# A triangular inverse in 32x32 array tiles, with part of a convolution moved to ScalarE and GpSimd

## The reference

```python
m = jnp.where(strict, jnp.einsum('bhncd,bhnsd->bhncs', k_beta, k) * decay, 0.0)
rhs = jnp.concatenate([v_beta, k_beta * jnp.exp(g)[..., None]], axis=-1)
sol = lax.linalg.triangular_solve(m + jnp.eye(C, dtype=jnp.float32), rhs, left_side=True, lower=True,
                                  unit_diagonal=True)
u = sol[..., :Dv]
w = sol[..., Dv:]
```

```python
y = val * jax.nn.sigmoid(gate)
y = causal_depthwise_conv(y, dw) + dw_bias.astype(y.dtype)
mu = jnp.mean(y32, axis=-1, keepdims=True)
var = jnp.mean(jnp.square(y32 - mu), axis=-1, keepdims=True)
```

## Time and profile before

| | |
|---|---|
| median of 3 runs | 2652.47 us (2650.78 to 2653.61) |
| the profiled execution | 2650.35 us, its span 2648.6 us |
| TensorE matmuls | 2560.8 us busy, 97% of the span |
| TensorE weight loads | 2027.1 us, 77% |
| VectorE | 1530.4 us, 58% |
| ScalarE | 1089.3 us, 41% |
| GpSimd | 114.6 us, 4% |
| granted TensorE clock, mean | 0.987 |

### The profile page before, as it was taken

How to read it: one execution, slowest core, us unless ns; L and a number is a source line. 1 busy time by engine, 2 the same in 40 slices (tenths; PEclk the granted TensorE clock), 3 DMA queues, 4 the chain that set the end, 5 groups by cost and what they waited for, 6 DMA issues and landing times.

```text
span 2648.6 us, 36760 instructions
## 1 busy us (share of the span) xinstructions
PE 2560.8 (97%) x12966; PEld 2027.1 (77%) x12966; DVE 1530.4 (58%) x1981; ACT 1089.3 (41%) x1570; POOL 114.6 (4%) x103
## 2 busy tenths in 40 slices
PE   7999999999999999999998899999899989899998
PEld 5767888887668888886687778888676778688886
DVE  4656755756566736646975554344559865543444
ACT  4554433435554424432473443233423734432323
POOL 1000000000000000000210010000102100100000
PEclk9999999999999999999998999999999999999998
DMA  4203332333113333342220223333221201233333
GB/s 132 72 1 95 95 105 86 100 98 92 41 34 95 103 94 95 102 112 64 56 64 3 64 72 105 92 95 105 54 80 48 72 10 50 76 101 92 95 99 91
DMA packets 394592, 208.04 MB, mean 79 GB/s; under 512 B 9738, under 2 KB 392660, under 8 KB 394484
## 3 DMA queue, kind: packets, MB, share of 16 engines
q1 hardware_dynamic: 391396, 202.79, 26.5%
q0 software_dynamic: 2176, 3.06, 0.5%
q10 hardware_dynamic: 912, 0.77, 0.1%
HBM read 205.34 MB, written 2.10 MB: 78 GB/s over the span
## 4 chain that ended last, share of the span: by engine, by line
PE 88%; DVE 6%; ACT 3%; issue 1%; DMA 0%; POOL 0%; DVEq 0%; SPq 0%; ACTq 0%; POOLq 0%
PE ps L611 64%; PE ps L630 6%; PE ps L888 2%; ACT whi L1437 1%; DVE ps L2758 1%; DVE x_sb L2761 1%; PE ps L1041 1%; PE ps L1056 1%; DVE yc L2467 1%; PE ps L943 1%; PE ps L675 1%; PE ps L945 1%; PE ps L1216 1%; PE ps L944 1%; ACT lnt L1441 1%
## 5 line engine op out<-in xcount | busy, mean ns | idle before, releaser
L1437 ACT ACTIVATE whi<-raw 128x1024 fp32r<-128x1024 f32 (+1 forms) x354 | 395.8, 1119 | 1062.9 <-PE ps L611 947.6
L611 PE MATMUL ps<-h_hi,whi 128*128 128x512 f32 x1984 | 788.3, 397 | 4.7 <-ACT whi L1437 4.1
L611 PE MATMUL ps<-h_lo,whi 128*128 128x512 f32 x1984 | 772.7, 389 | 0.0
L611 PE MATMUL ps<-h_hi,wlo 128*128 128x512 f32 x1984 | 530.3, 389 | 0.0
L2065 DVE TENSOR_TENSOR wlo<-raw,whi 128x1024 fp32r<-128x1024 f32 (+1 forms) x354 | 458.5, 1296 | 55.5 <-ACT whi L1437 54.5
L611 PEld LDWEIGHTS ps<-h_hi,whi 128*128 128x128 f32 x1984 | 372.7, 188 | 89.6 <-ACT whi L1437 8.2
L611 PEld LDWEIGHTS ps<-h_lo,whi 128*128 128x128 f32 x1984 | 372.7, 188 | 82.5 <-issue 6.2
L611 PEld LDWEIGHTS ps<-h_hi,wlo 128*128 128x128 f32 x1984 | 372.4, 188 | 77.1
L611 PE MATMUL ps<-a_hi,whi 128*128 128x512 f32 x592 | 230.3, 389 | 0.0
L611 PE MATMUL ps<-a_lo,whi 128*128 128x512 f32 x592 | 230.3, 389 | 0.0
L2793 DVE TENSOR_TENSOR cv<-ps,rstd 128x512 f32<-128x512 f32 x88 | 60.9, 692 | 247.8 <-PE ps L611 241.0
(11 more groups left out here) (406 smaller groups left out, 3235.5 us busy)
## 6 DMA issues: line engine op xcount, KB each, us to landing
raw<-in_w_up SPq DMA_DIRECT2D x132, 512.0 KB, 3.8
raw<-in_w_down SPq DMA_DIRECT2D x64, 704.0 KB, 4.5
raw<-in_w_in SPq DMA_DIRECT2D x82, 512.0 KB, 3.8
raw<-in_w_gate SPq DMA_DIRECT2D x44, 512.0 KB, 3.8
raw<-in_w_o SPq DMA_DIRECT2D x16, 512.0 KB, 3.6
raw<-in_w_out SPq DMA_DIRECT2D x16, 512.0 KB, 3.7
xs<-in_x SPq DMA_DIRECT2D x2, 1024.0 KB, 6.7
out<-xs SPq DMA_DIRECT2D x3, 512.0 KB, 2.9
```

Source lines behind the costliest of these rows:

```text
L611: return pe.matmul(ps[:, ACC[s], :], w[s][:, k, :], r[:, k, :], start=start, stop=stop)
L1437: act.activation(whi[s][:, 0:kt, :], raw[s][:, 0:kt, :], ACT.Copy).then_inc(w_hi_ready.sem, 1)
```

## The change

TensorE: in steps 2 to 15 each stage of the inverse covers only the four diagonal 32x32 blocks of the 128 partitions, as 4 chunks x 4 products of 32x32 with 32 columns each, in place of 4 x 2 of 64x64 with 64. Steps 0 and 1 keep the 64-wide form, and so do levels 5 and 6. Level 5 is updated in `xdT` in place like the levels before it, in one VectorE instruction, and ScalarE copies the result into the diagonal blocks of `xT` in two halves per head, at n = 18, 19, 22 and 23; the products that follow the loop wait for it.

The last eight taps: those of channel tile 0 stay on VectorE, 2, 3 and 3 behind heads 0, 1 and 2, none in the loop. Those of tile 1 are divided: ScalarE multiplies the shifted input by the tap (n = 0 to 7, into the two halves of `kb`), and GpSimd adds each product to `yc`, one after another, after its work for head 3.

Waits: GpSimd's scaling of the queries of a head now also waits for `head_masked` of that head (`lt0_ready`). VectorE's wait for ScalarE's copies ahead of L2505 is gone. The sums, copies and subtractions of the layer norm and of the attention output move two to six iterations forward.

```diff
--- before.py
+++ after.py
@@ -106,6 +106,8 @@
...
     LEVELS, HB = 7, P // 2
+    beside = [3, 3, 3, 2, 2, 2, 2, 2, 1, 1, 1, 1]
+    TAPS_IN = sum(beside)
     N_IN2 = 3 * NA + 2 * NC + 4 * GH
@@ -231,6 +233,8 @@
...
         p1_ready, x_new, xpt_ready = (sem(n, STEPS) for n in ("p1_ready", "x_new", "xpt_ready"))
+        late_tapped, diag_kept = again(qkstat_ready, CT - TAPS_IN - 1), again(qkrs_ready, GH)
+        tap_scaled = again(vvsq_ready, CT - TAPS_IN)
         p1_masked, p1_turned, low_zeroed = sem("p1_masked", STEPS - GH), sem("p1_turned", GH), again(qksq_ready, 1)
@@ -577,6 +581,7 @@
...
                     pool.wait_ge(qk_ready.sem, qk_ready.at(L, h))
+                    pool.wait_ge(lt0_ready.sem, lt0_ready.at(L, h))
                     nc.gpsimd.tensor_tensor(gq[:, h, :], gq[:, h, :], eg[:, h % 2, :], ALU.mult).then_inc(gq_scaled.sem, 1)
@@ -589,6 +594,12 @@
...
                         nc.gpsimd.memset(xT[:].rearrange("p h (t d) -> p (h t) d", d=P)[:, :, 0:HB], 0.0).then_inc(low_zeroed.sem, 1)
+                for n in range(CT - TAPS_IN):
+                    pool.wait_ge(tap_scaled.sem, tap_scaled.at(L, n))
+                    if n >= 1:
+                        pool.wait_ge(late_tapped.sem, late_tapped.at(L, n - 1))
+                    nc.gpsimd.tensor_tensor(yc[:, 1, :], yc[:, 1, :], kb[:, n % 2, :], ALU.add)\
+                        .then_inc((late_tapped if n < CT - TAPS_IN - 1 else dw_ready).sem, 1)
                 for c in range(1, NCH - 1):
@@ -1171,6 +1182,13 @@
...
+                def blocks(n, tb):
+
+                    size = P // 4 if 2 <= n < STEPS - 2 * GH else HB
+                    for p0 in range(0, P, size):
+                        c0 = tb * HB + p0 % HB
+                        yield slice(p0, p0 + size), slice(c0, c0 + size), slice(tb * P + p0, tb * P + p0 + size)
+
                 def level_first(n):
@@ -1189,9 +1207,8 @@
...
                         if n < STEPS - GH:
-                            for r in range(2):
-                                rows_r, diag_c = block(r, tb, P)
-                                mm = pe.matmul(ps[rows_r, ROT[n % 2], c], gv[rows_r, h, diag_c], xd[rows_r, h, c], start=True, stop=True)
+                            for rows_r, at, diag_c in blocks(n, tb):
+                                mm = pe.matmul(ps[rows_r, ROT[n % 2], at], gv[rows_r, h, diag_c], xd[rows_r, h, at], start=True, stop=True)
                         else:
@@ -1211,11 +1228,10 @@
...
                         if n < STEPS - GH:
-                            for r in range(2):
-                                rows_r = slice(HB * r, HB * (r + 1))
-                                mm = pe.matmul(ps[rows_r, ACC[n % 2], c], p1c[rows_r, n % 2, c], xdT[rows_r, h, c], start=True, stop=True)
+                            for rows_r, at, _ in blocks(n, tb):
+                                mm = pe.matmul(ps[rows_r, ACC[n % 2], at], p1c[rows_r, n % 2, at], xdT[rows_r, h, at], start=True, stop=True)
                         else:
-                            mm = pe.matmul(ps[0:HB, ACC[n % 2], c], p1c[HB:P, n % 2, c], xT[HB:P, h, tb * P + HB:(tb + 1) * P],
+                            mm = pe.matmul(ps[0:HB, ACC[n % 2], c], p1c[HB:P, n % 2, c], xdT[HB:P, h, c],
                                            start=True, stop=True)
@@ -1231,18 +1247,17 @@
...
                         if n < STEPS - 2 * GH:
-                            for r in range(2):
-                                rows_r = slice(HB * r, HB * (r + 1))
-                                mm = pe.matmul(ps[rows_r, STAT[n % 2], c], xdT[rows_r, h, c], ident[rows_r, rows_r], start=True, stop=True)
+                            for rows_r, at, _ in blocks(n, tb):
+                                mm = pe.matmul(ps[rows_r, STAT[n % 2], at], xdT[rows_r, h, at], ident[rows_r, rows_r], start=True, stop=True)
                         else:
-                            mm = pe.matmul(ps[0:HB, STAT[n % 2], c], xT[0:HB, h, tb * P:tb * P + HB], ident[0:HB, 0:HB], start=True, stop=True)
+                            mm = pe.matmul(ps[0:HB, STAT[n % 2], c], xdT[0:HB, h, c], ident[0:HB, 0:HB], start=True, stop=True)
                     mm.then_inc(xt_turned.sem, 1)
...
                     pe.wait_ge(turned_used.sem, turned_used.at(L, GH - 1))
+                    pe.wait_ge(dw_ready.sem, dw_ready.at(L, NC - 1))
                     for i in range(NC):
-                        pe.wait_ge(dw_ready.sem, dw_ready.at(L, i))
                         mm = pe.matmul(ps[:, TRN[0], :], ones[:], yc[:, i, :], start=(i == 0), stop=(i == NC - 1))
@@ -1257,9 +1272,9 @@
...
                         head_turned(GH - 1)
-                    if n == 15:
+                    if n == 13:
                         mean_sum()
-                    if n == 21:
+                    if n == 19:
                         centered_sum()
@@ -1268,6 +1283,7 @@
...
                     pe.wait_ge(x_new.sem, x_new.at(L, STEPS - GH + h))
+                    pe.wait_ge(diag_kept.sem, diag_kept.at(L, h))
                     if h == 0:
@@ -1876,16 +1892,34 @@
...
-                    if n in (13, 14):
-                        merged_high(n - 13)
-                    if n == 16:
+                    if n < CT - TAPS_IN:
+                        if n >= 2:
+                            act.wait_ge(late_tapped.sem, late_tapped.at(L, n - 2))
+                        else:
+                            act.wait_ge(kk_ready.sem, kk_ready.at(L, GH - 2 + n))
+                        k = TAPS_IN + n
+                        order.told(act.activation(kb[:, n % 2, :], ypad[:, 1, k:k + SEQ], ACT.Identity,
+                                                  scale=param(pd, L, D_DW + k * NC + 1)), tap_scaled, L, n)
+                    for h in {18: (0,), 19: (1,), 22: (2,), 23: (3,)}.get(n, ()):
+                        for r in range(2):
+                            rows_r = slice(HB * r, HB * (r + 1))
+                            ins = act.activation(xT[rows_r, h, :].rearrange("p (t d) -> p t d", d=P)[:, :, rows_r],
+                                                 xdT[rows_r, h, :].rearrange("p (t d) -> p t d", d=HB), ACT.Copy)
+                            if r == 0:
+                                order.step(ins)
+                            else:
+                                order.told(ins, diag_kept, L, h)
+
+                    if n in (8, 9):
+                        merged_high(n - 8)
+                    if n == 14:
                         act.wait_ge(mean_ready.sem, mean_ready.at(L, 0))
                         order.told(act.activation(lnt[:], ps[:, TRN[0], :], ACT.Copy, scale=1.0 / CC), mean_kept, L, 0)
-                    if n == 19:
+                    if n == 17:
                         for i in range(NC):
...
                             order.told(act.activation(msq2[:, i % 2, :], yc[:, i, :], ACT.Square), lnsq, L, i)
-                    if n == 22:
+                    if n == 21:
                         act.wait_ge(lnsq_used.sem, lnsq_used.at(L, NC - 1))
@@ -2501,7 +2535,6 @@
...
                     dve.wait_ge(kk_ready.sem, kk_ready.at(L, h))
-                    dve.wait_ge(turned_used.sem, turned_used.at(L, h))
                     order.told(dve.tensor_tensor(gv[:, h, :], ps[:, STAT[0], :], dm[:, s, :], ALU.mult), intra_made, L, h)
@@ -2537,17 +2570,8 @@
...
                     order.settle()
-                    if n < STEPS - 2 * GH:
+                    if n < STEPS - GH:
                         order.told(dve.tensor_tensor(xdT[:, h, :], xdT[:, h, :], ps[:, ACC[n % 2], 0:TB * HB], ALU.subtract), x_new, L, n)
-                    elif n < STEPS - GH:
-                        for r in range(2):
-                            rows_r = slice(HB * r, HB * (r + 1))
-                            ins = dve.tensor_tensor(by_token(xT[rows_r, h, :])[:, :, rows_r], by_block(xdT[rows_r, h, :]),
-                                                    by_block(ps[rows_r, ACC[n % 2], 0:TB * HB]), ALU.subtract)
-                            if r == 0:
-                                order.step(ins)
-                            else:
-                                order.told(ins, x_new, L, n)
                     else:
@@ -2555,18 +2579,15 @@
...
                 unit_blocks = lev[:, LEVELS - 1, :].unsqueeze(1).to_broadcast([P, TB, HB])
-                beside = [3, 3, 3, 2, 2, 2, 2, 2, 1, 1, 1, 1]
-                TAPS_IN = sum(beside)
-                assert 2 * (CT - TAPS_IN) == 16
-                LATE = ((0, 2), (2, 6), (6, 10), (10, 10))
+                LATE = ((0, 2), (2, 5), (5, 8), (8, 8))
                 def late_tap(n):
-                    k, t = TAPS_IN + n // NC, n % NC
-                    order.settle()
-                    ins = dve.scalar_tensor_tensor(yc[:, t, :], ypad[:, t, k:k + SEQ], param(pd, L, D_DW + k * NC + t), yc[:, t, :],
+                    k = TAPS_IN + n
+                    order.settle()
```

(13 more changed lines are left out.)

## The result

| | before | changed |
|---|---|---|
| median | 2652.89 us (4 runs, 2650.78 to 2653.61) | 2675.27 us (4 runs, 2674.18 to 2676.45) |
| the profiled execution | 2650.35 us, span 2648.6 | 2675.03 us, span 2673.2 |
| granted TensorE clock, mean | 0.987 | 0.976 |
| first mask to last copy, first and second inverse | 47.7 and 45.1 us | 60.6 and 58.8 us |

The changed kernel is slower by 22.4 us, a ratio of 1.0088 (95% interval 1.0072 to 1.0104). The forecast was 2633.8, with a range of 2622 to 2656.

The account below looks back on a forecast made before the run. Bound: chain 88% TensorE; edited part, the triangular inverse, paced by VectorE, then TensorE. Loops 10.1 and 7.5 less, head phase 1.4 twice: 20.4, less clock 1.7: 18.7 off 2650.35, 2631.7; plus 2.1 for the median, 2633.8 us, range 2622 to 2656.

Parts of the forecast that it names:

- The step that failed: TensorE's instruction fetches in the loop: pieces of about 1.0 us each, wanted one per 1.5 us, taken as hidden.
- My own sign of being wrong: In the loop: TensorE's issue waits between stages, or starts of different tiles 0.025 us or more apart, would refute the forecast.
- The rival on the slow side: Inverse loop: the number of matmuls sets a stage, 0.93 us; 20 us a layer more than forecast, 2674; chance 0.15.
- The rival that did name instruction supply: Inverse loop: instruction supply or dispatch keeps a stage at 0.47 us; 2 us a layer lost, 2638; chance 0.15.
- Price of a 32x32 stage: TensorE stage in the inverse: 8 rounds of 0.03, 0.25 us in place of 0.47; upper bound 0.93.
- Head phase: Ahead of the loop: waits and a tap removed save 1.4 us a layer, between ends of 0 and 3.8.
- The collision: Head phase: GpSimd's products of 1.27 and 1.50 us meet VectorE's taps and L2524; at head 2 about 0.9 lost.
- Loop: Inverse from first mask M: mask 3 at M+5.0, 10 at M+12.8, 19 at M+28.4; 37.6 us a layer with tail.
- Tail: End of the inverse loop after mask 19: second channel sum 1.9, 13 stages of 0.47, copies and hops, 9.2 us.
- Level 5: Level 5 in place saves VectorE 0.42 us a step, hidden behind TensorE at 64 wide.
- Clock: TensorE idler in the new loop: one more low stretch of 3.4 us, half of it lost, 1.7 us.
- My sign: In the loop: the granted clock at 0.50 for more than 7 us would show the forecast wrong.

Follow-up runs that it names:

- the probe: The changed kernel in 64x64 tiles plus two independent streams behind its last transposes, 256 fp32 products of 32x32, then 128 of 64x64: 2655.79 us, one run.
- 64x64 version: The changed kernel with 64x64 products in place of the 32x32 ones, taps, waits and level 5 as changed: 2640.36 us, ratio 0.995 to before.
- half the blocks: The changed kernel with only two of the four 32x32 blocks of each stage, half of levels 1 to 4 left out: 2641.84 us, ratio 0.9961.
- the filler: The changed kernel in 64x64 tiles with 16 one-column bf16 products of 32x32 added to every stage of steps 2 to 15: 2788.6 us, ratio 1.0513.

## Why the prediction was wrong

**The step that failed** is the last before the rivals: "The loop wants them some two to three times as often, one per 1.5 us: hidden if that latency is all there is." From the earlier trace rows I took the time of a piece's transfer, 1.0 us, and not the rate of pieces, and put the cost of more instructions at nothing. From the start of a transfer to TensorE's next matmul it is 2.4 to 2.8 us in the first inverse of the changed kernel, and the next transfer did not start early enough to hide that. The rows that I needed were there: the 64x64 steps ran at 99 instructions per 1.40 us, 71 per us. I had no evidence for a higher sustained rate, and the change asked for 195 in 1.1 to 1.4 us; I even called that "a density that no row has", but used it only against the array. Measured is one piece per 3.4 to 4.1 us, however much more is asked. 195/67 gives 2.9 us a step; from mask 4 to mask 9 the changed kernel takes 2.93 and 2.74. The new issue waits, 31.8 us, and the two channel sums at the low clock (3.71 and 3.40 instead of 1.91: 3.3) make 35.1, of 34.9 between the two forms of the change; that it closes this well is partly luck, since stage lengths differ too. My own sign of being wrong, issue waits of TensorE between stages, is what came true.

**The rival on the slow side** gave 2674, but by another cause. It wanted 0.029 us between any two matmuls on the array; measured are 0.003 to 0.007 between starts on different tiles, 0.30 for a stage of 32. The floor of about 25 ns in the Trainium skill (TensorE: Matmul & The Clock Gate, "Wait — 56ns, not 53.3ns?") does not hold across tiles, as the earlier trace rows had suggested; within one of the probe's bursts 128 matmuls start in 1.45 us, 0.011 each. The rival that did name instruction supply let it keep a stage at 0.47: right in kind, wrong in size (2638), because it did not count that the number of instructions doubles while the supply was already used up.

**Price of a 32x32 stage**, 0.25: measured 0.30 at the full clock, with rounds of 0.032 against the estimated 0.03. A small miss that no longer mattered.

**Head phase**, 1.4 a layer: 1.15 came between the last low part and the first mask. The collision stood where I placed it. In the changed kernel L2557 waits out GpSimd's product, while the mask of the last head, 1.82 before, has its 0.87:

```profile
1390.95 1.27 DVE L2557 TENSOR_TENSOR gk<-lev,gk 128x256 f32<-128x256 bf16 x1
...
1394.26 0.87 DVE L2545 TENSOR_TENSOR gk<-gv,lev 64x256 f32<-64x256 f32 x2
```

Between the low parts of the last three weight tiles, ahead of that, another 2.4 us were gained in the first layer and 2.0 in the second. The run with the head waits alone has 0.1 and 1.2 of this, so 2.3 and 0.8 are left for the two taps taken away behind heads 1 and 2, of which the sum had one. In all it is 3.6 and 3.2, near the upper bound of 3.8 (whose terms add up to 3.7).

**Loop**, first inverse, counted from the first mask M. I had mask 3 at M+5.0: 5.3. Mask 10 at M+12.8: 24.8, but 15.4 in 64x64, and 15.1 with half the blocks (13.5 in the second inverse). In the 64x64 version the adds of GpSimd do go 1.4 apart (six in 8.35 us), but the steps there take 1.40, not the 1.12 that 7.8 for seven steps means: TensorE's three stages fill them. With half the blocks masks 4 to 7 of the second inverse come at 1.08 to 1.11, so taps and adds do not hold the loop; the instructions do, soon after. Mask 19 at M+28.4: 49.9 (31.3 in 64x64). Tail 9.2: 10.7 in both. So without the stalls the loop is 42.0, not 37.6: the taps' gain was real but mis-sized by 4.

**Level 5** I costed at nothing, as hidden behind TensorE. It was not hidden in steps 17 and 18, where VectorE had the subtractions as well.

**Clock**, 1.7 us in all: the changed kernel runs 27.3 and 23.9 us of its loops at 1.2 GHz. My sign, the clock at 0.50 for over 7 us of the loop, came true, together with the stalls.

**The sum** of the two profiles: loops 13.0 and 13.7 longer, head phases 3.6 and 3.2 shorter, which makes 19.9 of 24.6. The rest lies where no instruction differs; 3.3 us of it ahead of the second block's first head phase, where the 64x64 version and the run with the head waits are late by 3 to 4 us as well, but the run with tiles in one stage not at all. So this part differs between runs whose code is the same there, and is not put down to the change.

## What to carry to other kernels

Count instructions per microsecond, loads and matmuls and waits, before cutting products smaller, and compare with the densest stretch that the trace has. A denser form than any on record is not to be put down as free: here the old form stood near the top rate already and left little room for a finer one, however cheap each product is on the array. The sign of a short supply here was "issue" waits of 1.5 to 2.5 us that come at an even spacing, fall inside a group of equal instructions, and name no engine. When a form saves array time by doubling instructions, look for a stage of the old form with few instructions per microsecond, and try it there first.

## What the runs showed of the hardware

- TensorE got 16384 bytes of instructions, 256 of them, every 3.4 to 4.1 us where it wanted more, and took 65 to 73 per us over ten steps; the transfer of a piece itself took 0.9 to 1.4 us. In the probe the next piece began to move at 2633.81, when the last matmul of the burst started (2633.76), and work resumed at 2636.03, 2.2 us later; the two pieces behind it began 0.3 and 0.5 us before the last start of their burst, and work resumed 2.6 us after they began. What sets off a transfer these traces do not show.
- Where it wanted less, pieces came less often: 8 to 9 us apart in the loop with the filler, at 30 instructions per us.
- Once it has them TensorE can take them much faster: 256 in 1.45 us between first and last start, over 170 per us.
- Matmuls of 32x32 on four tiles start 6 to 7 ns apart at 1.2 GHz and 3 to 7 ns at 2.4; a round of four takes 0.053 and 0.032 us.
- Alternating four 64x64 fp32 matmuls with four 32x32 bf16 ones costs 0.55 us a pair at the low clock, more than twice the plain round, and TensorE shows as busy all the time, at a clock of 0.50.
